# Attention outputs written already transposed, gated-linear-attention levels two at a time, and a finer start

## The reference

```python
# first block
y_a = diff_attention(q_a, k_a, v_a, lam, subln_w, lambda_init)
y_b = neighbourhood_attention_2d(q_b, k_b, v_b, rpb)      # 8 heads of 64
merged = g_a * (y_a @ w_branch_a) + g_b * (y_b @ w_branch_b)
x = x + rmsnorm(merged @ w_out, post_mix_w)
x = x + rmsnorm((silu(h @ w_gate) * (h @ w_up)) @ w_down, post_ffn_w)
# second block
y_a = mla(c_q, c_kv, k_rope, ...) @ mla_w_o               # 8 heads of 64, causal
y_b = gla(g_q, g_k, g_v, g_lr, g_og, ...) @ gla_w_o       # 4 heads
h = h + (sigmoid(gate_a) * y_a + sigmoid(gate_b) * y_b) @ w_out
h = h + (silu(u @ ffn_w_gate) * (u @ ffn_w_up)) @ ffn_w_down
```

```python
diff = bc[:, :, :, None, :] - bc[:, :, None, :, :]
decay = jnp.exp(jnp.where(causal[:, :, None], diff, -jnp.inf))
attn = jnp.einsum('bhid,bhjd,bhijd->bhij', qc, kc, decay)
o_intra = jnp.einsum('bhij,bhje->bhie', attn, vc)
```

## Time and profile before

| | us |
|---|---|
| median of 3 runs | 766.02 |
| lowest and highest | 766.01, 766.63 |
| profiled execution, its own time | 766.46 |
| its span from first to last instruction | 764.70 |
| TensorE busy (3897 matmul records) | 757.3 |
| DVE, ACT busy | 475.5, 402.6 |
| granted clock of TensorE, mean | 0.999 |

### The profile page before, as it was taken

How to read it: one execution, slowest core, us unless ns; L and a number is a source line. 1 busy time by engine, 2 the same in 40 slices (tenths; PEclk the granted TensorE clock), 3 DMA queues, 4 the chain that set the end, 5 groups by cost and what they waited for, 6 DMA issues and landing times.

```text
span 764.7 us, 10244 instructions
## 1 busy us (share of the span) xinstructions
PE 757.3 (99%) x3897; PEld 629.6 (82%) x3897; DVE 475.5 (62%) x712; ACT 402.6 (53%) x598; POOL 55.7 (7%) x130
## 2 busy tenths in 40 slices
PE   9999999999999999999999999999999999999997
PEld 7887888888888888888898788888888888888886
DVE  5586756576846565775285796555765665656633
ACT  5646766444744444554378563666355454544522
POOL 1100100000370000000023000200002000000000
PEclk9999999999999999999999999999999999999999
DMA  8856353546656556645475373352555655655641
GB/s 314 262 187 215 122 175 119 177 168 196 198 172 208 186 167 197 196 161 193 139 247 168 102 240 115 111 162 87 191 172 161 219 170 167 213 184 153 214 137 56
DMA packets 57199, 134.32 MB, mean 176 GB/s; under 512 B 7815, under 2 KB 13246, under 8 KB 57150
## 3 DMA queue, kind: packets, MB, share of 16 engines
q1 hardware_dynamic: 56640, 132.40, 53.6%
q10 hardware_dynamic: 510, 1.27, 0.5%
HBM read 132.60 MB, written 1.05 MB: 175 GB/s over the span
## 4 chain that ended last, share of the span: by engine, by line
PE 97%; ACT 1%; DVE 1%; DMA 1%; issue 0%; SPq 0%; POOL 0%; ACTq 0%; POOLq 0%
PE acc L1060 85%; PE aux L992 4%; PE aux L1172 2%; PE aux L1121 1%; PE aux L1151 1%; PE aux L1244 1%; PE aux L1139 1%; PE acc L1051 1%; DMA weights_raw<-in_w_in_dram 1%; ACT weights_high L667 0%; PE aux L1282 0%; PE aux L1051 0%; PE aux L1274 0%; DVE silu_tmp L1452 0%; DVE silu_tmp L1449 0%
## 5 line engine op out<-in xcount | busy, mean ns | idle before, releaser
L1060 PE MATMUL acc<-weights_high,h_high 128*128 128x512 f32 (+1 forms) x720 | 232.3, 398 | 0.5 <-ACT h_high L675 0.4
L1331 DVE SCALAR_TENSOR_TENSOR weights_low<-weights_raw,gain_columns,weights_high 128x1024 fp32r<-128x1024 f32 (+3 forms) x189 | 218.5, 1190 | 14.8 <-ACT weights_high L667 14.5
L1060 PE MATMUL acc<-weights_high,h_low 128*128 128x512 f32 (+1 forms) x720 | 224.6, 388 | 0.0
L1060 PE MATMUL acc<-weights_low,h_high 128*128 128x512 f32 (+1 forms) x720 | 224.0, 387 | 0.0
L667 ACT ACTIVATE weights_high<-weights_raw,gain_columns 128x1024 fp32r<-128x1024 f32 (+3 forms) x188 | 195.3, 1075 | 18.4 <-DMA weights_raw<-in_w_in_dram 8.2
L1060 PEld LDWEIGHTS acc<-weights_low,h_high 128*128 128x128 f32 x720 | 134.4, 188 | 28.2
L1060 PEld LDWEIGHTS acc<-weights_high,h_low 128*128 128x128 f32 x720 | 134.2, 188 | 28.0 <-DVE h_low L1350 0.4
L1060 PEld LDWEIGHTS acc<-weights_high,h_high 128*128 128x128 f32 x720 | 129.3, 188 | 27.4 <-issue 4.3
L1328 DVE TENSOR_TENSOR weights_low<-weights_raw,weights_high 128x1024 fp32r<-128x1024 f32 x68 | 81.0, 1220 | 34.8 <-ACT weights_high L667 34.7
L667 ACT ACTIVATE weights_high<-weights_raw 128x1024 fp32r<-128x1024 f32 x68 | 69.5, 1057 | 45.9 <-DMA weights_raw<-in_ffn_w_down_dram 21.3
L1791 POOL TENSOR_SCALAR stats<-stats 128x1 f32<-128x1 f32 (+1 forms) x15 | 7.7, 512 | 618.0 <-ACT row L680 286.4
...
## 6 DMA issues: line engine op xcount, KB each, us to landing
...
```

Of the source, the lines that this page charges most:

```text
L1060: i = nc.tensor.matmul(acc[:, 2 * t + b, 0:width], lhs[:, k0, sl], w[:, u % RING, base + d:base + d + width], start=(kt == 0 and n == 0), ...
L1331: i = nc.vector.scalar_tensor_tensor(lo[:, u % RING, c], raw[:, u % RING, c], gcol[:, g:g + 1], hi[:, u % RING, c].bitcast(F32), ALU.mult, ...
```

## The change

Three parts of the program are written differently.

**1. na and mla.** A new DVE step `share` takes the reciprocal of the row sums and multiplies the probabilities by it (two operations of up to 128 x 256), before they are transposed. `turn_p` waits for it. In `pv`, 64 columns of v are now stationary and the 128 columns of `probs_T` stream; the two heads of a pair go to the left and the right half of the array in turn and write the lower and the upper 64 partitions of the bank. What comes out is already transposed: ACT copies it to `y_high`, DVE subtracts into `y_low`, and the `turn_y` of na and mla (four insertions of four transposes, with their L675 and L1350) is gone.

**2. The levels of gla.** The diagonal is computed on DVE by a new step `gla_diag` in slot 2 (product of q and k, sum per head, and two multiplications with the mask that also fill `gla_attn_parts`, so that its memset on POOL is gone). The six other levels are multiplied in three visits of two levels, in slots 4, 8 and 12, where before seven visits of one level stood in slots 2, 3, 4, 6, 8, 10 and 12. The `gla_keys` and `gla_decay` steps stay in about the same slots.

**3. The start.** Seven logical fill matmuls in place of eight. The first quarter of x is transposed into two banks, and DVE casts and subtracts it in halves of 128 x 256. x(1,0) is transposed behind the first pass of the first item and no longer behind the second. The load of the first strip's left half is issued by ACT's queue behind its first small load, so that SP's right half, x(1,0) and all that follow move up by one place in SP's queue; seven small loads and the table load of ACT stand behind one more issue.

```diff
+        q[11 + e].append(do("share", "na", i))
         q[12 + e].append(do("turn_p", "na", i))
         q[13 + e] += [do("pv", "na", i), do("heads_out", "na", i)]
-        if i % 4 == 3:
-            q[22 + i // 4].append(do("turn_y", "na", i // 4))
...
-    for n, slot in enumerate((2, 3, 4, 6, 8, 10)):
-        g[slot] = [do("gla_level", n), do("gla_keys", n)] + ([do("gla_decay", n + 2)] if n + 2 < len(LEVELS) else [])
+    g[2] = [do("gla_diag"), do("gla_keys", 0), do("gla_decay", 2)]
+    g[3] = [do("gla_keys", 1)]
+    g[4] = [do("gla_levels", 0), do("gla_keys", 2), do("gla_decay", 3)]
     g[5] = [do("rope_k")]
+    g[6] = [do("gla_keys", 3), do("gla_decay", 4)]
     g[7] = [do("decay_k")]
+    g[8] = [do("gla_levels", 1), do("gla_keys", 4), do("gla_decay", 5)]
     g[9] = [do("decay_q")]
+    g[10] = [do("gla_keys", 5)]
     g[11] = [do("gla_state")]
-    g[12] = [do("gla_level", len(LEVELS)), do("attn_blocks")]
+    g[12] = [do("gla_levels", 2), do("attn_blocks")]
     g[13] = [do("gla_output", 0)]
     g[14] = [do("gla_output", 1)]
     g[15] = [do("gla_heads", 0)]
...
         m[i + 2].append(do("score", "mla", i))
+        m[i + 3].append(do("share", "mla", i))
         m[i + 4].append(do("turn_p", "mla", i))
         m[i + 5] += [do("pv", "mla", i), do("heads_out", "mla", i)]
-        if i % 4 == 3:
-            m[i + 7].append(do("turn_y", "mla", i // 4))
     m = [order(slot) for slot in m]
...
-            sp.dma_start(raw[:, 0, 0:512], dram["w_in"][0, 0:P, 0:512]).then_inc(*tick("first_loaded", None, 16))
...
                         marks["sumsq", ("da", qt)] = counts["sumsq"]
+                elif kind == "heads_out" and a[0] in TILED:
+                    kind, i = a
+                    qt, n = divmod(i, 4)
+                    act.wait_ge(*at("pv_done", (kind, i)))
+                    nc.scalar.activation(yT[0][:, {"na": 4, "mla": 0}[kind] + n, qt * P:(qt + 1) * P],
+                                         aux[bank_of[kind, i]][:, 0:P], ACT.Copy)\
...
             load_gains("pre_mix_w")
+            act.dma_start(raw[:, 0, 0:512], ins["w_in"][0, 0:P, 0:512]).then_inc(*tick("first_loaded", None, 16))
...
-                        pe.wait_ge(*at("turned_high_vec" if (name, t) == ("qk_a", 0) else "turned_high", (tag, t, 0)))
+                        if (name, t) == ("qk_a", 0):
+                            pe.wait_ge(*at("turned_high_vec", "mix_first"))
+                        else:
+                            pe.wait_ge(*at("turned_high", (tag, t, 0)))
...
-                    if u == 0 and t == 0 and w is lo:
+                    if u == 0 and t == 0 and lhs is xl:
 
...
+                        if (tag, t, b) == ("mix", 0, 0):
+                            turn("mix_first", 1, slices(src[:, 0, 0:256], 2), ("turned_low", "mix_first"))
+                            turn((tag, t, b), 0, slices(src[:, 0, 256:512], 2), ("turned_low", (tag, t, b)))
+                            continue
...
-                    pe.wait_ge(*at(*((("vec", ("combined", i)) if kind == "da" else ("probs", (kind, i))))))
+                    pe.wait_ge(*(at("vec", ("combined", i)) if kind == "da" else at("vec", ("share", kind, i)) if kind in TILED else
+                                  at("probs", (kind, i))))
...
+                    for kt in range(kts):
+                        for hb in range(2):
+                            c = (2 * n + hb) * HD
+                            m = nc.tensor.matmul(aux[bank][hb * HD:hb * HD + HD, 0:P], v[:, kt, c:c + HD],
                                                  probs_T[kind][:, i % 2, hb * 256 + kt * P:hb * 256 + (kt + 1) * P],
-                                                 v[:, kt, c], start=(kt == 0), stop=(kt == kts - 1))
...
+                                                 start=(kt == 0), stop=(kt == kts - 1))
+                            if kt == kts - 1:
+                                m.then_inc(*tick("pv_done", (kind, i)))
+                    reader[bank] = ("turned_low", ("heads", kind, i))
...
+                elif kind == "gla_levels":
...
+                    banks_ = (2 * (j % 2), 2 * (j % 2) + 1)
...
+                    for n in (2 * j, 2 * j + 1):
+                        pe.wait_ge(*at("vec", ("level_k", n)))
+                        e = EDs[n % 3]
+                        for hb, b in enumerate(banks_):
...
+                    m.then_inc(*tick("gla_done", ("levels", j)))
+                    for b in banks_:
+                        reader[b] = ("vec", ("level", 2 * j + 1))
...
-            fill_zeros(8)
+            fill_zeros(7)
...
+                            parts = ((0, 1, "mix_first"), (2, 0, (tag, t, b)))
+                            for k, bank, key in parts:
+                                dve.wait_ge(*at("turned", key))
+                                signal(nc.vector.tensor_copy(hT[0][:, k:k + 2, 0:P], aux[bank][:, 0:2 * P]
+                                                             .rearrange("p (k s) -> p k s", k=2)),
+                                       "turned_high_vec", key)
+                            for k, bank, key in parts:
+                                dve.wait_ge(*at("turned_high_vec", key))
...
+                elif kind == "share":
...
+                    keys = att_keys(kind, i)
+                    T = probs[kind][:, i % 2, :]
+                    dve.wait_ge(*at("probs", (kind, i)))
                     r = stat(("sum", kind, qt), 8)[:, 2 * n:2 * n + 2]
                     then(nc.vector.reciprocal(r, r))
...
+                    for hb in range(2):
+                        p = T[:, hb * 256:hb * 256 + keys]
+                        nc.vector.tensor_scalar(p, p, r[:, hb:hb + 1], None, ALU.mult)\
+                            .then_inc(*tick("vec", ("share", kind, i)))
+                elif kind == "heads_out" and a[0] in TILED:
...
+                    dve.wait_ge(*at("turned_high", ("heads", kind, i)))
+                    k, s = {"na": 4, "mla": 0}[kind] + n, slice(qt * P, (qt + 1) * P)
+                    nc.vector.tensor_tensor(yT[1][:, k, s], aux[bank_of[kind, i]][:, 0:P], yT[0][:, k, s].bitcast(F32),
+                                            ALU.subtract).then_inc(*tick("turned_low", ("heads", kind, i)))
...
-                        marks["vec", ("y", kind, qt)] = counts["vec"]
+                        marks["turned_low", ("y", kind, qt)] = counts["turned_low"]
...
+                elif kind == "gla_diag":
...
+                    dve.wait_ge(*at("acc_act", ("gla_qk", TOKS - 1)))
+                    flat = rt.rearrange("p a h b d -> p (a h b d)")
+                    then(nc.vector.scalar_tensor_tensor(
+                        flat.rearrange("p (t f) -> p t f", t=TOKS), gqk[:, :, 0:256], GLA_DK ** -0.5,
+                        gqk[:, :, 256:512], ALU.mult, ALU.mult))
+                    dot = stat("gla_diag", 8)
+                    then(nc.vector.tensor_reduce(dot, flat.rearrange("p (k d) -> p k d", d=GLA_DK), AX.X, ALU.add))
+                    dve.wait_ge(*at("pool", "level_masks"))
+                    mask = lmask[:, 0, :].rearrange("p (o s) -> p o s", o=1).to_broadcast([P, 4, GLA_CHUNK])
                     for hb in range(2):
-                        i = nc.vector.copy_predicated(
-                            AC[:, hb, :, :].rearrange("p k (b s) -> p k b s", s=w)[:, :, :, upper],
-                            mask.to_broadcast(shape),
-                            aux[2 * (n % 2) + hb][:, 0:256].rearrange("p (k b s) -> p k b s", k=4, s=w)[:, :, :, upper])
-                        i.then_inc(*tick("vec", ("level", n)))
+                        nc.vector.tensor_tensor(AC[:, hb, :, :], mask,
+                                                bcast(dot.rearrange("p (k b) -> p b k", b=2)[:, hb, :], GLA_CHUNK),
+                                                ALU.mult).then_inc(*tick("vec", "diag"))
+                elif kind == "gla_levels":
+                    j, = a
+                    dve.wait_ge(*at("gla_done", ("levels", j)))
+                    for n in (2 * j, 2 * j + 1):
...
+                        for hb in range(2):
+                            i = nc.vector.copy_predicated(
+                                AC[:, hb, :, :].rearrange("p k (b s) -> p k b s", s=w)[:, :, :, upper],
+                                mask.to_broadcast(shape),
+                                aux[2 * (j % 2) + hb][:, c:c + 256]
+                                .rearrange("p (k b s) -> p k b s", k=4, s=w)[:, :, :, upper])
+                            i.then_inc(*tick("vec", ("level", n)))
...
-                    then(g.memset(AT[:, :, :, :, :, :].rearrange("p a b c d e -> p (a b c d e)"), 0.0))
-                    done(g.memset(AC[:, :, :, :].rearrange("p a b c -> p (a b c)"), 0.0), "pool", "attn_zero")
+                    done(g.memset(AT[:, :, :, :, :, :].rearrange("p a b c d e -> p (a b c d e)"), 0.0), "pool", "attn_zero")
```

104 lines of the change are left out of this document (46 added, 58 removed).

## The result

| | before | changed |
|---|---|---|
| median of 4 runs, us | 766.33 | 762.30 |
| lowest and highest | 766.01, 766.64 | 762.18, 762.51 |
| profiled execution, its own time | 766.46 | 762.25 |
| its span | 764.70 | 760.5 |
| TensorE records | 3897 | 3847 |

A forecast was written before the change was run, and what follows sets the result against it. TensorE was taken as the bound, busy 757.3 of 764.7 us. The terms -2.3 - 1.8 + 0 - 2.6 + 0.5 - 0.5 = -6.7 gave 759.3 us against the median of 766.02; range 757.2 to 761.9 (88%).

The forecast's parts named there:

- What moves to DVE and ACT: In na and mla, share and copies end before turn_p needs them, slack 1.0 and 0.7 us in na: no cost.
- The term for the levels: gla's seven visits at 7.8 us become three of 1.71; the diagonal fits DVE's idle 2.56 us: -2.6 us.
- rival (e): One projection's low strips come late for several items: 762 to 764.5 us, chance 4%.
- The tail: Behind gla's last level visit, four copies instead of two make TensorE wait before the first output: +0.5 us.
- pv, turn_y and levels: TensorE insertions: pv of na -2.3, pv of mla 0.0, turn_y of na and mla -1.8, gla's levels -2.6 us.
- The start: Halved conversions, one fill fewer, earlier right half and x(1,0) bring the first items forward: -0.5 us (-0.2 to -1.0).
- (b): Share late at turn_p in all 12 slots of na and mla; at 0.7 us each, 767.7 us, chance 2%.
- my signs of being wrong: Pairs over 0.11 apart, turn_p of na or mla waiting, new low-strip waits at L1060, or first-strip halves no earlier than 7.31.
- a sign of being right: No new line among TensorE's waits, apart from 0.3 to 0.6 us before gla's first output.
- (a): In pv of na and mla the array halves don't overlap: 765.4 us, chance 3%.
- (c): Two levels of a visit side by side, best start, tail 0.2 less: 757.6 us, chance 12%.
- (d): Dearer halved mode in mla and na, levels in full series, smaller start gain, late low strips: 761.4 us, chance 17%.

The follow-up runs named there:

- experiment 9: Changed kernel with share ahead of heads_out, rope_k in slot 3, decay_k in slot 9, own banks and signal per level: 758.79 us; with left half by SP: 758.94.
- Experiments 1 and 2: Each from the changed kernel: share ahead of heads_out on DVE, 760.74 us; ACT's copies of the heads ahead of the gates' sigmoid in two na slots, 761.6 us.
- Experiment 1: Changed kernel with share ahead of the heads' low parts (heads_out) on DVE in each slot: 760.74 us.
- Experiment 5: Changed kernel with gla's levels as before (diagonal on TensorE, seven visits of one level): 763.67 us.
- experiments 3 and 4: Each from the changed kernel, in gla: decay_k moved from slot 7 to 9, 762.35 us; rope_k moved from slot 5 to 3, 760.93 us.
- experiment 8: Changed kernel with pv's loops swapped, so four records go to the left half of the array, then four to the right: 763.02 us.
- the nine traces: Traces of the changed kernel and eight follow-up runs, all with the left half loaded by ACT's queue; against before, their starts won 0.88 to -0.07 us.

## Why the prediction was wrong

The direction, the mechanisms of the gain and the terms on TensorE were right. The kernel of experiment 9, without the three waits, takes 758.8 us; it has also lost the wait before gla's output (0.53), which the forecast had, and with that it would be 759.3, the forecast. That it meets the tenth is luck, since the start alone moves by more. The failed step is the part **What moves to DVE and ACT**, with its result "so this costs nothing", and what the sum left out behind it.

- **na (+0.95).** The part says "ACT ends its strip at 110.45 and copies two heads". In the trace of before, ACT has the gates' sigmoid at 110.83, between that strip and the next:

```profile
110.83 1.06 ACT L707 ACTIVATE gates<-gates 128x1024 f32<-128x1024 f32 x1 [0.38 <-DVE gates L1407]
```

  I had placed the copies in a free moment of ACT and not behind all that ACT's list has before them. DVE waited 1.35 us for those copies, more than the slack of 1.0 and 0.7 us. Experiments 1 and 2 show it from both sides. The multiplications took 0.35 us each, but the next began 0.27 behind the one before, for the 0.28 that I took from the earlier trace rows; the size was right.
- **mla (+0.75).** "In mla one i has a slot, half the work": true, and beside the point. y_low waits for ACT's copy, which stands behind ACT's exponentials of another i and a strip (L669, 520.98 for 1.04 us), and DVE's own next share and exponentials stand behind y_low. In the changed kernel, DVE and then TensorE:

```profile
522.22 0.29 DVE L1660 TENSOR_TENSOR y_low<-aux,y_high 128x128 fp32r<-128x128 f32 x1 [2.27 <-ACT y_high L859]
```

```profile
525.74 0.66 PE L1204 MATMUL aux<-probs_T,v_latent 128*64 128x128 f32 x8 [0.39 <-ACT probs_T L837]
```

  DVE idled 2.27 us over something that nobody needed soon. Experiment 1 removed all of it.
- **437 to 451 us (+1.22).** The term for the levels priced TensorE's visits and asked only whether the diagonal fits into DVE's pause, which it did. It did not ask who is late next when TensorE no longer spends 1.1 us in slots 2, 3 and 6 each. The rows for it stood in the trace of before: DVE without a pause from 444.78 to 455.04, and gate_a2's first record at 455.14, 0.05 after it could have started. The slack was nearly zero. In slot 6 TensorE gained 1.1 us and DVE lost only two copies, so the gain of one visit came back as a wait. Experiment 5 shows that this wait belongs to the levels, experiments 3 and 4 that it hangs on DVE's list. The time fell into the interval of rival (e), to which I gave 4%, but not by its mechanism: no low strip was late, an accumulator was.
- **The tail (+0.60 for +0.5)** and **pv, turn_y and levels**: right, the levels by 0.1 better than taken. The per-visit cost follows from the alignment: a visit of two levels costs 0.6 more than one of one. Priced like the earlier trace rows, from 466.80 to 469.42 less 0.91, the last one cost 1.71, the figure that I had.
- **The start (-0.72 for -0.5)**: the size was off by 0.22 in this trace, and by about as much the other way on average over the nine traces (-0.33). The table load came not 0.4 but 0.7 us later (4.32), and what I had not seen is that the landing of the left half moves by up to 1.0 us from run to run (5.5 to 6.5).
- **The rivals.** (b), share late at turn_p, was the mechanism that struck, with the place right and the price wrong: two slots of na by 0.47 and mla by 0.75 in all, not twelve slots alike. I had judged it by the size of share's operations, where what counts is what share stands behind. One of my signs of being wrong stood in the profile, turn_p of na waited, and a sign of being right was missing: TensorE had new lines among its waits, for a projection and for mla's pv. (a) fell with experiment 8, the extra overlap of (c) with the visits at 1.71, the dearer mode of (d) with the 0.35 us.
